# Two DMA queues for the expert weights: w2 requested by GpSimd, w1 by SyncE

## The reference, cut to what matters

```python
def expert_block(args):
    tok_b, e = args
    xb = xpad[tok_b]
    hu = xb @ w1[e] + b1[e]                 # w1[e]: 1024 x 2048
    x_glu = jnp.minimum(hu[:, 0::2], SWIGLU_LIMIT)
    x_lin = jnp.clip(hu[:, 1::2], -SWIGLU_LIMIT, SWIGLU_LIMIT)
    act = x_glu * jax.nn.sigmoid(SWIGLU_ALPHA * x_glu) * (x_lin + 1.0)
    return act @ w2[e] + b2[e]              # w2[e]: 1024 x 1024
```

## Time and profile before

| what | us |
|---|---|
| median of 3 runs | 1372.37 (1371.92 to 1373.81) |
| profiled execution, its own time | 1369.29 |
| its span | 1367.2 |
| PE busy | 1276.1 (93% of the span) |
| DVE / ACT / POOL busy | 392.3 / 187.4 / 52.6 |
| DMA queue q1 (SyncE's), share of 16 engines' span | 83.3% |
| chain that ended last | PE 52%, DMA 43% |

### The profile page before, as it was taken

One profiled execution on the slowest core, in us unless ns is written; L12 is line 12 of the kernel. 1 busy time (PEld: TensorE's weight loads), 2 busy tenths in 40 slices (PEclk: granted clock), 3 DMA queues, 4 the chain that ended last, 5 costly groups with the idle time before them and its releaser, 6 DMA issues.

```text
span 1367.2 us, 17275 instructions
## 1 busy us (share of the span) xinstructions
PE 1276.1 (93%) x6449; PEld 612.4 (45%) x6450; DVE 392.3 (29%) x981; ACT 187.4 (14%) x399; POOL 52.6 (4%) x48
## 2 busy tenths in 40 slices
PE   4999999999989999998999998999999998999996
PEld 1788878898743333323333322333333322333322
DVE  1698565732152121111211111211211111211112
ACT  2000213422030010000110000100110000110002
POOL 0220003220000000000000000000000000000000
PEclk9999999999989999999999999999999999999999
DMA  9998550009348999999999999699999999999994
GB/s 374 366 328 301 186 185 1 1 2 338 123 150 333 428 426 427 427 425 425 426 428 427 426 428 423 256 427 425 426 429 425 427 429 423 425 426 430 425 426 200
DMA packets 65525, 471.67 MB, mean 345 GB/s; under 512 B 3997, under 2 KB 4314, under 8 KB 31706
## 3 DMA queue, kind: packets, MB, share of 16 engines
q1 hardware_dynamic: 64672, 469.61, 83.3%
q10 hardware_dynamic: 538, 1.13, 0.3%
q0 software_dynamic: 288, 0.55, 0.2%
HBM read 470.23 MB, written 1.05 MB: 345 GB/s over the span
## 4 chain that ended last, share of the span: by engine, by line
PE 52%; DMA 43%; SPq 2%; DVE 1%; ACT 1%; issue 1%; DVEq 0%
DMA ring<-in_exp_w_dram 41%; PE bank L1261 17%; PE bank L778 13%; PE bank L1287 6%; PE bank L1161 2%; PE bank L950 2%; PE bank L1232 2%; DMA ring<-in_w_in_dram 2%; SPq L479 2%; PE bank L1299 1%; PE bank L1083 1%; PE bank L1253 1%; PE bank L1067 1%; PE bank L1080 1%; PE bank L823 0%
## 5 line engine op out<-in xcount | busy, mean ns | idle before, releaser
L1261 PE MATMUL bank<-ring,work 128*64 128x512 f32 x2112 | 472.3, 598 | 48.9 <-DMA ring<-in_exp_w_dram 48.8
L1261 PEld LDWEIGHTS bank<-ring,work 128*64 128x64 f32 x2112 | 144.9, 137 | 372.6 <-issue 273.2
L1287 PE MATMUL bank<-ring,work 128*64 128x512 f32 x1056 | 233.9, 595 | 0.0
L778 PE MATMUL bank<-region_h,ring 128*128 128x256 f32 x704 | 156.4, 383 | 4.6 <-DMA ring<-in_w_in_dram 4.6
L778 PEld LDWEIGHTS bank<-region_h,ring 128*128 128x128 f32 x704 | 134.0, 192 | 23.6 <-DMA ring<-in_w_in_dram 5.1
L1287 PEld LDWEIGHTS bank<-ring,work 128*64 128x64 f32 x1056 | 72.8, 137 | 137.5 <-issue 137.5
L735 ACT ACTIVATE work<-work 128x256 f32<-128x256 f32 x66 | 27.5, 416 | 765.2 <-DVE work L1754 765.2
L1754 DVE TENSOR_SCALAR work<-bank 128x256 f32<-128x256 f32 x66 | 27.6, 419 | 347.9 <-PE bank L1261 347.9
L1781 DVE TENSOR_TENSOR work<-bank,work 128x512 f32<-128x512 f32 x33 | 22.8, 691 | 315.7 <-PE bank L1287 315.7
L1299 PE MATMUL bank<-work 64*128 64x512 f32 x264 | 65.6, 615 | 0.8 <-DVE work L1781 0.8
L1232 PE MATMUL bank<-qkv,work 128*64 128x512 f32 x272 | 65.7, 605 | 0.6 <-DVE work L1694 0.6
(11 more groups left out here) (297 smaller groups left out, 877.1 us busy)
## 6 DMA issues: line engine op xcount, KB each, us to landing
ring<-in_exp_w_dram SPq DMA_DIRECT2D x192, 2048.0 KB, 23.7
ring<-in_w_in_dram SPq DMA_DIRECT2D x13, 2048.0 KB, 13.1
ring<-in_ada_w_dram SPq DMA_DIRECT2D x12, 2048.0 KB, 13.7
ring<-in_w_gdn_out_dram SPq DMA_DIRECT2D x2, 2048.0 KB, 9.9
ring<-in_w_out_dram SPq DMA_DIRECT2D x2, 2048.0 KB, 15.3
ring<-in_w_pool_out_dram SPq DMA_DIRECT2D x1, 2048.0 KB, 8.1
region_x<-in_x_dram SPq DMA_DIRECT2D x2, 512.0 KB, 4.4
region_x<-in_x_dram ACTq DMA_DIRECT2D x2, 512.0 KB, 5.7
```

Source lines behind the costliest of these rows:

```text
L778: mm = nc.tensor.matmul(out_ap, w(k) if w else w_slot(n, j, k), rhs[:, k, :], start=(k == 0), stop=(k == kc - 1))
L1261: mm = nc.tensor.matmul(bank[b][h * SLOTS:(h + 1) * SLOTS, :], xT[:, c % 4, c // 4, :], slot_as(q, 2)[:, i, lo:lo + 512], start=False, sto ...
L1287: mm = nc.tensor.matmul(bank[2][o * SLOTS:(o + 1) * SLOTS, :], actT[:, b, c, h, :], slot_as(4 + b, 2)[:, h, lo:lo + 512], start=(b + h + c ...
```

## The change

GpSimd, after its last piece of mixer work, takes over the requests for w2_0 and w2_1 of every expert, in its own DMA queue. It has its own loop over the experts, with its own read of `first_block_of`. The transfers are the same in size and layout, and wait for the same `used[4]` and `used[5]`. They raise new semaphores, `w2_in[0]` and `w2_in[1]`, for which `w2_chunk` waits. SyncE's loop keeps slots 0 to 3.

```diff
+        w2_in = [sem(f"w2_in{i}") for i in range(2)]
...
-            def stream(e, blocks_before):
-                for s in range(RING):
-                    src = w1_dram[e, :, 2 * s:2 * s + 2, :] if s < 4 else w2_dram[e, s - 4]
+            def stream_w1(e, blocks_before):
+                for s in range(4):
                     sp.wait_ge(used[s], blocks_before + USES)
-                    sp.dma_start(slot_as(s, 2), src).then_inc(landed[s], 16)
-
-            stream(0, 0)
+                    sp.dma_start(slot_as(s, 2), w1_dram[e, :, 2 * s:2 * s + 2, :]).then_inc(landed[s], 16)
+
+            stream_w1(0, 0)
...
             with sp.Fori(1, E) as e:
-                stream(e, first_block_of(sp, e))
+                stream_w1(e, first_block_of(sp, e))
...
+            def stream_w2(e, blocks_before):
+                for b in range(2):
+                    pool.wait_ge(used[4 + b], blocks_before + USES)
+                    pool.dma_start(slot_as(4 + b, 2), w2_dram[e, b]).then_inc(w2_in[b], 16)
+
+            stream_w2(0, 0)
+            pool.wait_ge(vec_route, 1)
+            with pool.Fori(1, E) as e:
+                stream_w2(e, first_block_of(pool, e))
...
-                pe.wait_ge(landed[4 + b], 16 * (e + USES + 1))
+                pe.wait_ge(w2_in[b], 16 * (e + 1))
```

## The result

| | before | changed |
|---|---|---|
| median of the runs, us | 1372.1 (4 runs) | 1392.3 (4 runs, 1391.5 to 1394.0) |
| profiled execution, own time / span | 1369.3 / 1367.2 | 1394.0 / 1392.1 |
| ratio to before (95% interval) | | 1.0151 (1.0131 to 1.0171) |

The change costs 20 us: slower, as forecast, inside the range of 1376 to 1403, but by a third more than the 15.2 us of the sum, and just above the 1380 to 1391 of the main account. The profiled pair lies 24.9 us apart in span, since its before was among the shortest and its after the longest of their runs; sums made on the traces go by 24.9.

The account below looks back on a forecast made before the run. The prediction took DMA transfers to bound most of the loop, with issue costs zero. w1_3 landing 7.6 us later at the two-block expert and at the end summed to +15.2 us, 1372.4 to 1387.6 us, range 1376 to 1403.

Parts of the forecast that it names:

- the 15.2 us of the sum: Lateness of w1_3, 7.6 us each at the expert with two blocks and at the end, added to the old time.
- the main account: Forecast of 1380 to 1391 us from w1_3 landing later at two places; chance 0.43.
- What bounds the kernel: From about 532 to 853 us and 1017 us to the end, transfers bound it: periods of 29.52 us, 425 to 430 GB/s.
- Issue and semaphores at zero: Moving 64 requests from SyncE to GpSimd and replacing semaphores one for one costs zero, since issue time is hidden.
- GpSimd's queue goes in front of waiting w1 transfers: In the loop, requested w2 takes rate from w1 queued earlier; cited: 7.2 us to land against 27.0.
- Two places, each once: Late w1_3 costs 7.6 us at the expert with two blocks and 7.6 us at the end, nothing in mid-run.
- Equal halves of the rate: While both queues have work each gets half, so w1_3 lands 2.2 us before an expert's last bytes instead of 9.84.
- the forecast's own alternative: Packet-by-packet turns give w2 a third; PE waits up to 5.7 us at w2_1; 3.9 to 9.6 us each place.
- w2 going first altogether: Extreme share in which w1_3 lands last, 9.84 us late at each place: 1392; extreme shares together have chance 0.25.
- What would show it: Signs expected in the trace: w2 landing times, PE's waits, double-block gap, last w1_3 against last bytes, unchanged DMA rate.
- w2 lands as late as w1: Sign that the prediction is wrong; in the loop w2 was expected to land in about 10 to 15 us, not 24.7.
- waits at L1287 appear that make periods longer than 29.5 us: Sign that the prediction is wrong: PE waiting at the w2 matmuls long enough to lengthen the loop's periods.

Follow-up runs that it names:

- sem_only: Kernel of before, SyncE still requesting all six chunks in one queue, but w2 arrivals raise two semaphores of their own; 0.9999 of before.
- Split late: Changed kernel with two queues only for experts 16 to 31 and the first; experts 1 to 15 in SyncE's queue in order; 1.0091 of before.
- split early: Changed kernel with two queues only for experts 0 to 15; experts 16 to 31 in SyncE's queue in order; 1.0102 of before.
- w1_8k: Changed kernel with each w1 chunk requested as two DMAs of rows of 8 KB instead of one of 16 KB; 1.0154 of before, 1392 us.
- split_filled: Changed kernel with four extra matmuls of resident data (8 records) between w2_0 and w2_1 of every block; 1.0127 of before.

## Why the prediction was right, and where it fell short

- **What bounds the kernel**: right. The rate of the loop stayed at 424 to 428 GB/s in nearly every slice, and 22.5 of the 24.9 us stand at the places at which the DMA engines stand still.
- **Issue and semaphores at zero**: right (sem_only 0.9999; all requests from GpSimd 1.0022, with the 3 us at the start). GpSimd needs 0.72 us for one of these requests; the forecast had 0.93 from its nearest row.
- **GpSimd's queue goes in front of waiting w1 transfers**: right, and shown by packets.
- **Two places, each once**: right, and the best part of the forecast. Split late and split early separate them.
- **Equal halves of the rate**: this step failed. "I take halves, near the middle" set aside the row that it cites, from which packets of 16 and 8 KB give a third. Measured were 33 to 39% for w2. At such a share PE no longer waits at w1_3 but at w2_1, by 5 to 7 us at about every third expert; the forecast's own alternative ("between 3.9 and 9.6 at each place") describes it. w1_8k shows that with real halves the waits do go to w1_3, and that the 15.2 us of the sum are near what halves cost (13.3 us).
- **The size**: 7.6 us at each place was forecast, 11.5 and 11.0 us stand in the traces. Half-clock matmuls are 2.1 and 2.7 of these. Without them 9.4 and 8.3 are left, inside the 3.9 to 9.6 that the forecast has for a third and near the upper end. The term that was missing altogether is the clock: the forecast treated PE's waits as free wherever the DMA engines are the bound, and asked only when PE resumes, not how fast. That 1392 also stands in the forecast, for w2 going first altogether, is chance: w2 did not go first.
- **What would show it**: gap "about 20" was 23.5; w2 landing in "10 to 15 us" was 16.1 in the median, 29.8 at most; waits "at w1_3 alone" was wrong; that the last w1_3 starts "only 2 us before" the last bytes was wrong, since PE comes from the last wait at w2_1, in the block before, and runs through: its w1_0 starts at 1352.6, so w1_3 at about 1363.0, 2.4 us behind the last bytes. That "w2 lands as late as w1" was named as a sign of being wrong, and it came: 16.1 us for w2 against 14.8 for w1. It was badly chosen, since with two requests fewer in front w1 lands sooner too (24.7 before). That "waits at L1287 appear that make periods longer than 29.5 us" was another sign. The waits did appear, but three experts still take 88.6 us (1256.72 to 1345.30 in the chain shown above), 29.5 each, so on average the periods held. By their rows PE's waits in a period of before are 2.3 us (1.03 and 1.25); the 2.7 of the forecast is the difference of two block times, and nothing rests on it.

## What to carry to other kernels

A stream that is consumed in a fixed order and is bound by transfers belongs in one queue, if it behaves as here: a second one added no rate and took the turn of what is needed first, with a share that follows the size of its packets. Look for the price not in the steady loop, where total bytes rule, but where the transfers wait for the consumer (here a repeated block and the end), for each such place pays the lateness once. And ask of a wait not only how long it is but how fast the engine is behind it.

## What the runs showed of the hardware that I had not expected

- Nine waits of 5 to 7 us cost TensorE more than their own length: the granted clock fell from 1.00 to 0.50, and the 16 records behind took 5.3 to 6.5 us instead of 3.65, though 43 waits of about 1 us, nearly the same sum, had left it at 1.00. Between them lie waits of both kinds: 5.35 us behind waits of 2.12 and 2.13 us (split_filled), 3.65 behind one of 2.89 us (changed kernel).
- The loop's rate depends on how a chunk is cut even at this size: about 426 GB/s with w1 in rows of 16 KB and one request of 2 MiB, a steady 422 with rows of 8 KB and two requests of 1 MiB, 8 us over the kernel.
- Extra work on TensorE need not cost anything: 8 more records in each of 33 blocks made the changed kernel no slower that can be told (1.0127 of before, against 1.0151 without them).
- Two busy queues took turns row by row, whichever engine owned the queue with the longer rows: 80 and 80 packets in 4 us both ways round, so that the longer rows got 61 to 62% of the engines' time.
